# A decoder layer on one core: fillers in the router's chain, an earlier last scatter, high parts first in two units, x by two queues

## The reference

```python
h = h + HybridMixer(rms_norm(h, g1))       # gated linear attention + dilated window attention
h = h + MemXAttn(rms_norm(h, g2), mem)     # 4 heads, 256 memory tokens
h = h + MoE(rms_norm(h, g3))               # top 4 of 32 experts, router with bias
out = rms_norm(h, final_g)
```

## Time and profile before

| | us |
|---|---|
| median of 3 runs (lowest, highest) | 1241.34 (1241.11, 1243.54) |
| the profiled execution's own time | 1242.41 |
| its span, first to last instruction | 1240.7 |
| PE busy, share of the span | 1153.2, 93% |
| DVE busy | 411.6, 33% |
| ACT busy | 261.6, 21% |
| mean rate of all transfers, GB/s | 369 |
| mean granted clock of TensorE, 1 is 2.4 GHz | 0.986 |

### The profile page before, as it was taken

The page is one execution under the profiler, slowest core; times in us unless marked ns, Lnnn a source line. Parts: engine busy times, 40 slices in busy tenths (PEclk is TensorE's granted clock), DMA queues, the critical chain, the costliest instruction groups (busy, mean ns, idle before and its releaser), DMA issues.

```text
span 1240.7 us, 16139 instructions
## 1 busy us (share of the span) xinstructions
PE 1153.2 (93%) x6687; PEld 576.8 (46%) x6687; DVE 411.6 (33%) x803; ACT 261.6 (21%) x450; POOL 20.9 (2%) x40
## 2 busy tenths in 40 slices
PE   8999999999999999999989887998998898889887
PEld 7888989887433333333323232432332233224322
DVE  6789474665422222222122112211221122122112
ACT  5655464464400010010001000100110010001001
POOL 4000000000000000000000000000000000000000
PEclk9999999999899999999999999999999999999999
DMA  8455524986699999999999999999999999999996
GB/s 329 173 204 183 190 76 182 382 316 244 239 420 395 430 418 434 429 435 428 435 427 435 430 433 429 431 429 432 431 431 433 431 431 431 435 428 435 419 419 264
DMA packets 30117, 458.38 MB, mean 369 GB/s; under 512 B 3584, under 2 KB 3600, under 8 KB 8816
## 3 DMA queue, kind: packets, MB, share of 16 engines
q1 hardware_dynamic: 28800, 454.57, 87.8%
q0 software_dynamic: 832, 2.51, 0.6%
q10 hardware_dynamic: 432, 0.55, 0.1%
HBM read 456.57 MB, written 1.05 MB: 369 GB/s over the span
## 4 chain that ended last, share of the span: by engine, by line
PE 61%; DMA 29%; SPq 3%; issue 2%; ACT 2%; DVE 2%; POOL 0%; DVEq 0%; ACTq 0%; POOLq 0%
PE bank L1888 22%; DMA ring<-in_w_down 16%; DMA ring<-in_w_gate_up 12%; PE bank L1910 10%; PE bank L1495 4%; PE bank L1472 4%; PE sums L1553 3%; PE sums L1472 3%; SPq L431 3%; PE sums L1839 3%; PE sums L1495 2%; PE bank L1829 2%; PE bank L1553 2%; PE bank L1901 2%; DMA ring<-in_w_dense 1%
## 5 line engine op out<-in xcount | busy, mean ns | idle before, releaser
L1888 PE MATMUL bank<-ring,reg_a 128*64 128x512 f32 x2016 | 457.9, 606 | 42.5 <-DMA ring<-in_w_gate_up 41.8
L1888 PEld LDWEIGHTS bank<-ring,reg_a 128*64 128x64 f32 x2016 | 142.4, 139 | 324.4 <-issue 263.4
L1910 PE MATMUL bank<-ring,reg_ol 128*64 128x512 f32 x1024 | 227.0, 595 | 14.5 <-DMA ring<-in_w_down 12.8
L1389 DVE TENSOR_TENSOR masks<-bank,bT 128x256 f32<-128x256 f32 x64 | 27.2, 424 | 449.7 <-PE bank L1901 449.7
L1910 PEld LDWEIGHTS bank<-ring,reg_ol 128*64 128x64 f32 x1024 | 79.2, 137 | 141.1 <-issue 133.8
L625 ACT ACTIVATE reg_t<-bank 128x512 f32<-128x512 f32 x64 | 38.2, 597 | 440.5 <-PE bank L1888 240.5
L969 DVE SCALAR_TENSOR_TENSOR ring<-ring 128x2048 f16<-128x2048 f32 x47 | 107.3, 2289 | 40.1 <-ACT ring L643 39.8
L643 ACT ACTIVATE ring<-ring 128x2048 f16<-128x2048 f32 x47 | 89.5, 1910 | 32.7 <-PE sums L1553 14.1
L926 ACT ACTIVATE masks<-masks 128x256 f32<-128x256 f32 x64 | 26.7, 417 | 326.4 <-DVE masks L1390 326.4
L1839 PE MATMUL sums<-reg_t,reg_g 64*128 64x512 f32 x256 | 70.1, 634 | 5.5 <-ACT reg_t L625 5.5
L1376 DVE COPY reg_t<-bank 128x512 f32<-128x512 f32 x32 | 22.1, 691 | 159.2 <-PE bank L1888 159.2
(11 more groups left out here) (323 smaller groups left out, 884.8 us busy)
## 6 DMA issues: line engine op xcount, KB each, us to landing
ring<-in_w_gate_up SPq DMA_DIRECT2D x52, 4096.0 KB, 29.8
ring<-in_w_down SPq DMA_DIRECT2D x26, 4096.0 KB, 30.8
ring<-in_w_dense SPq DMA_DIRECT2D x47, 1024.0 KB, 5.1
ring<-in_w_gate_up SPq DMA_DIRECT2D x10, 2048.0 KB, 9.6
ring<-in_w_gate_up SPq DMA_DIRECT2D x16, 1024.0 KB, 25.5
ring<-in_w_down SPq DMA_DIRECT2D x6, 2048.0 KB, 11.0
ring<-in_w_gate_up SPq DMA_DIRECT2D x16, 512.0 KB, 14.2
ring<-in_w_down SPq DMA_DIRECT2D x12, 512.0 KB, 7.2
```

The costliest lines, as they stand in the source:

```text
L1888: ins = mm(pt[nh][col:col + 64, :], xg[:, c, j * SLOTS:(j + 1) * SLOTS], loaded(v + i, C, c), start=(c == 0), stop=(c == C - 1))
L1910: ins = mm(pt[2][64 * nh:64 * nh + 64, :], actT[:, 4 * i + c, :], w[:, nh * 512:(nh + 1) * 512], start=(i == 0 and c == 0), stop=(i == 1 a ...
```

## The change

1. x is loaded by two queues: SP issues the first half, ACT the second, ahead of the vectors.
2. q_g gets two banks, one for each 128 of its columns: q_g as before and q_g1, which is listed after q_g in FILLS but is given bank 7 outside the turns. PE makes q_g and q_g1 together and k_g after them by passes instead of chunks: all high by high products, then those with the low activation, then those with the low weight, each pass waiting only for the parts that it reads. DVE makes all four low parts of x_T before the second piece of the first unit's cut. ACT empties q_g and q_g1 by two copies of half the size at the old place in its stream.
3. Seven products of 128x512 that nobody reads are put into bank 0 in the router: four after the sums are opened, three after "all".
4. For the last expert both halves of the scatter of the expert before it move ahead of its first product, and the first two of its units are loaded in four pieces instead of two. Three semaphores that had been used once are counted on for pieces.
5. In the final norm DVE multiplies the second tile's half by the gain first and asks for the first root before it multiplies the first; ACT's first square no longer waits for a gain.

```diff
@@ -88 @@
-FILLS = [f"x_T{i}" for i in range(4)] + ["q_g", "k_g", "alr", "v_g0", "v_g1", "r_g0", "r_g1", "lg"]
+FILLS = [f"x_T{i}" for i in range(4)] + ["q_g", "q_g1", "k_g", "alr", "v_g0", "v_g1", "r_g0", "r_g1", "lg"]
 FILLS += [f"q_d{g}{a}" for g in range(NG) for a in range(2)] + ["cum"]
@@ -111 @@
 LAST_FILL = {k: k for k in HALVES if k in FILLS}
-LAST_FILL.update({"gla0": "bg1", "dil0": "bd1", "gla1": "bg3", "dil1": "bd3", "xv1": "xv11",
+LAST_FILL.update({"q_g": "q_g1", "gla0": "bg1", "dil0": "bd1", "gla1": "bg3", "dil1": "bd3", "xv1": "xv11",
                   "xo0": "xo01", "xo1": "xo11"})
-_N = FILLS.index("f_T0")
-BANK = {f: 4 + SUMS.index(f) if f in SUMS else i % BANKS if i < _N else (i - _N + 2) % 4 for i, f in enumerate(FILLS)}
+_TURNED = [f for f in FILLS if f != "q_g1"]
+_N = _TURNED.index("f_T0")
+BANK = {f: 4 + SUMS.index(f) if f in SUMS else i % BANKS if i < _N else (i - _N + 2) % 4 for i, f in enumerate(_TURNED)}
+BANK["q_g1"] = BANKS - 1
 TURN = {f: sum(BANK[e] == BANK[f] for e in FILLS[:i]) for i, f in enumerate(FILLS)}
@@ -336 @@
         FIRST_PIECES = {10: 4, 11: 4, 12: 4, 13: 4, 14: 2, 15: 2}
-        LAST_PIECES = {UPE * (EG - 1) + i: n for i, n in enumerate((2, 2, 4, 4, 2, 4))}
+        LAST_PIECES = {UPE * (EG - 1) + i: n for i, n in enumerate((4, 4, 4, 4, 2, 4))}
         LAST_PIECES.update({UPE * (EG - 2) + i: 2 for i in range(UPE)})
         per_group = UPE * EG
...
+        once = [spare_ld] + extra_ld
+        piece_ld = {k: (once[i], 16) if i < len(once) else (sem(f"piece_ld{k[0]}_{k[1]}"), 0)
+                    for i, k in enumerate(counted)}
...
@@ -404 @@
             xt_src = A["x"][0].rearrange("(t p) d -> p t d", p=P)
-            for t in range(TT):
-                sp.dma_start(h[:, t, :], xt_src[:, t, :]).then_inc(ld_x[t], 16)
+            sp.dma_start(h[:, 0, :], xt_src[:, 0, :]).then_inc(ld_x[0], 16)
             def columns(v, e, o, n):
@@ -619 @@
             link = chain(act, act_chain)
+            act.dma_start(h[:, 1, :], A["x"][0, P:T, :]).then_inc(ld_x[1], 16)
             act.dma_start(vT[:], A["vecs"]).then_inc(ld_ahead, 16)
@@ -680 @@
                     act.wait_ge(trig_in, 2)
-                unscaled(dst.rearrange("p a b -> p (a b)"), b[:]).then_inc(free_bank(name), 1)
+                    unscaled(dst[:, 0, :], b[:, 0:T]).then_inc(free_bank(name), 1)
+                    unscaled(dst[:, 1, :], take(act, "q_g1")[:, 0:T]).then_inc(free_bank("q_g1"), 1)
+                else:
+                    unscaled(dst.rearrange("p a b -> p (a b)"), b[:]).then_inc(free_bank(name), 1)
             b = take(act, "alr")
@@ -932 @@
                 act.wait_ge(acc_full, 2 * t + 2)
-                act.wait_ge(fin_gain, t + 1)
+                if t:
+                    act.wait_ge(fin_gain, 1)
                 act.activation(xn[:, t, :], sums[t][:], ACT.Square, accum_out=st[:, 56 + t:57 + t]).then_inc(fin_ss, 1)
                 act.wait_ge(root_done, 7 + t)
+                act.wait_ge(fin_gain, 2 - t)
                 o = out_sb[:, t, 0:512]
@@ -1022 @@
             ahead_cut(0, AHEAD, ahead_act, 1, ahead_dve)
-            for q in range(2):
+            for q in range(4):
                 low_T("x_T", q, aT, vT[:, 0:8])
             ahead_cut(AHEAD, HALF, w_high, 1, w_low)
-            for q in range(2, 4):
-                low_T("x_T", q, aT, vT[:, 0:8])
             cut_ahead("q_g")
@@ -1108 @@
             emptied(dve, "q_g")
+            emptied(dve, "q_g1")
             emptied(dve, "k_g")
@@ -1427 @@
             dve.wait_ge(ld_late, 16 * 2)
-            for t in range(TT):
-                dve.wait_ge(acc_full, 2 * t + 1)
-                gained(t, 0)
-            for t in range(TT):
-                asked(t)
+            dve.wait_ge(acc_full, 3)
+            gained(1, 0)
+            asked(0)
+            gained(0, 0)
+            asked(1)
             for t in range(TT):
@@ -1512 @@
             norm_transposes("x_T", lambda t, c: xn[:, t, c * P:(c + 1) * P], ((norm_xn, 1), (norm_xn, 2)))
-            def first_ready(c):
-                pairs_ready("x_T")(c)
-                if c == 0:
-                    pe.wait_ge(ahead_dve, 2)
-                if c == C // 2:
-                    pe.wait_ge(w_low, 1)
-            feature_major("q_g", weights("q_g"), aT, C, chunk_ready=first_ready)
-            feature_major("k_g", weights("k_g"), aT, C)
+            def highs_first(outs, w, cols, before):
+                for k, (pw, px) in enumerate(PASSES):
+                    for c in range(C):
+                        before(k, c)
+                        for b, o in zip(outs, cols):
+                            ins = mm(b, w[:, pw, c, o:o + P], aT[:, px, c, :], start=(k == 0 and c == 0),
+                                     stop=(k == 2 and c == C - 1))
+                            if k == 2 and c == C - 1 and len(outs) > 1:
+                                filled(ins, ("q_g", "q_g1")[o // P])
+                return ins
+            def cut_of(name):
+                return cut[HALVES.index(name) % EARLY].rearrange("p k (c n) -> p k c n", n=width(name))
+            def first_parts(k, c):
+                if k == 0:
+                    pe.wait_ge(x_high, c + 1)
+                    if c % (C // 2) == 0:
+                        pe.wait_ge(*((w_high, 1) if c else (ahead_act, 1)))
+                elif k == 1:
+                    pairs_ready("x_T")(c)
+                elif c % (C // 2) == 0:
+                    pe.wait_ge(*((w_low, 1) if c else (ahead_dve, 2)))
+            def second_parts(k, c):
+                if c == 0 and k == 0:
+                    pe.wait_ge(w_high, 2)
+                if c == 0 and k == 2:
+                    pe.wait_ge(w_low, 2)
+            highs_first([fill(name)[:, 0:T] for name in ("q_g", "q_g1")], cut_of("q_g"), (0, P), first_parts)
+            b = fill("k_g")
+            for i in range(2):
+                ins = highs_first([b[:, i * T:(i + 1) * T]], cut_of("k_g"), (i * P,), second_parts)
+            filled(ins, "k_g")
             pe.wait_ge(consts, 7)
@@ -1781 @@
             pe.wait_ge(f_high, 1)
+            wide = f16[:, 0, 0, 0:4, :].rearrange("p c n -> p (c n)")
+            def awake(n):
+                emptied(pe, "rl1")
+                for _ in range(n):
+                    mm(rl[1][:], f16[:, 0, 0, 0, :], wide, start=True, stop=True)
             for name in SUMS:
-                filled(mm(fill(name)[:], f16[:, 0, 0, 0, :], f16[:, 0, 0, 0:4, :].rearrange("p c n -> p (c n)"),
-                          start=True, stop=False), name)
+                filled(mm(fill(name)[:], f16[:, 0, 0, 0, :], wide, start=True, stop=False), name)
+            awake(4)
             pe.wait_ge(gate_ready, 1)
@@ -1791 @@
             filled(mm(b[:, 0:E], ones[:], mask[:, 1, :], start=False, stop=True), "all")
+            awake(3)
             def gates_T():
@@ -1856 @@
                         scatter_matrices(i)
-                    else:
+                    elif not (last and j == EG - 1):
                         scatter(j - 1, (i,))
@@ -1924 @@
                         down_biases()
+                    if last and j == EG - 1:
+                        scatter(j - 1)
                     for i in range(2):
                         between(j, i)
```

More of the change, by code:

```diff
@@ L338, in _program @@
         FIRST_PIECES = {10: 4, 11: 4, 12: 4, 13: 4, 14: 2, 15: 2}
-        LAST_PIECES = {UPE * (EG - 1) + i: n for i, n in enumerate((2, 2, 4, 4, 2, 4))}
+        LAST_PIECES = {UPE * (EG - 1) + i: n for i, n in enumerate((4, 4, 4, 4, 2, 4))}
         LAST_PIECES.update({UPE * (EG - 2) + i: 2 for i in range(UPE)})
         per_group = UPE * EG
-        piece_ld = {(v, i): sem(f"piece_ld{v}_{i}") for v, n in LAST_PIECES.items() for i in range(n)
-                    if ORDER[v % UPE][0] != 1}
+        spare_ld, extra_ld = sem("spare_ld"), [sem(f"extra_ld{i}") for i in range(2)]
+        counted = [(v, i) for v, n in sorted(LAST_PIECES.items()) for i in range(n) if ORDER[v % UPE][0] != 1]
+        once = [spare_ld] + extra_ld
+        piece_ld = {k: (once[i], 16) if i < len(once) else (sem(f"piece_ld{k[0]}_{k[1]}"), 0)
+                    for i, k in enumerate(counted)}
         def piece_done(v, i):
             m = ORDER[v % UPE][0]
-            return (piece_ld[v, i], 16) if m == 2 else (piece_ld[v - m, i], 32)
-        spare_ld, extra_ld = sem("spare_ld"), [sem(f"extra_ld{i}") for i in range(2)]
+            done, already = piece_ld[v - m % 2, i]
+            return done, already + (16 if m == 2 else 32)
         def turn_of(v, z, first):
```

## The result

The changed kernel takes 1252.1 us (median of 4 runs, 1251.86 to 1253.12) against 1241.6 of the kernel before in the same comparison: 1.0083 times, 95% interval 1.0066 to 1.0101. It is slower by about 10 us. The profiled execution took 1252.17, its span 1250.4, which is 9.7 more than before.

What follows compares the result with a forecast made beforehand. Weight transfers set the end, but PE frees their slots, so a microsecond PE loses before the first expert moves the end by one. Terms sum to +7.45 on the profiled 1242.41: 1249.9, taken as 1249.7 against the median, range 1247.0 to 1253.8.

Steps and rivals of the forecast that it cites:

- the wait for bank 7: First units: v_g0 must wait until ACT empties q_g1, behind unit 4's cut and both sines: +8.75 us.
- rival (a): Router: the stall comes and the clock falls there all the same, so no -3.0: 1252.7 us, chance 0.22.
- the half clock: After PE's wait for the bank, v_g0's products run at 1.2 GHz: +2.2 us, bounds 1.8 to 3.4.
- unit 3's late release: First units: DVE's later second cut delays unit 3's load, with unit 4 behind it: +0.5 us, bounds 0 to +1.3.
- wait at r_g1 gone: First units: PE's old idle time ahead of r_g1 disappears because PE is late: -1.15 us.
- router, with the added products: Router: the clock stays high over gathers and first expert's products, -3.0 us; the added products cost +0.1.
- smaller pieces: Last expert: two more units loaded in quarters, at a slightly lower rate: +0.2 us, bounds 0 and 0.4.
- Rival (b): Not slower: the shift of PE's first units is made up behind it by the transfer stream: 1240.1 us, chance 0.09.
- High parts first: First units: PE ends k_g near 21.8 instead of 24.3, a gain of 2.5 us that reaches nobody.
- x by two queues: First units: x one issue earlier brings DVE's second cut to some 15.4; otherwise costs or gives nothing.
- (c): Stall and more: unit 4 late by 1.3, clock low for 6.8 us, later cuts chained: 1253 to 1255, chance 0.10.
- (d): The stall, but little of the clock loss and a better router: 1247.5 us, chance 0.07.

Runs made afterwards that it cites:

- a_drain: The changed kernel, but ACT empties q_g and q_g1 right after alr's cut, ahead of the cuts of units 3 and 4 and the sines: 1243.31 us.
- a_drain_dve: a_drain with DVE again cutting the first unit's second half between the second and third pair of low parts: 1240.0 us.
- a_mem: The changed kernel with POOL's load of mem issued after the masks, the bank still emptied at the old place: 1251.05 us.
- a_nofill: The changed kernel without the seven added products: 1254.93 us.
- a_p2: The changed kernel with the first two units of the last expert in two pieces again: 1253.43 us in one run.
- b_fill: The kernel before with the seven added products alone: 1239.09 us, 0.9977 times.
- b_tail: The kernel before with the moved scatter and the new final norm alone, without the pieces: 1242.69 us in one run.
- b_x2: The kernel before with only x's second half issued by ACT's queue, ahead of the vectors: 1242.7 us for 1241.74 before.
- b_fill_tail: The kernel before with the seven added products, the moved scatter and the new final norm: 1239.83 us, 0.9985 times.
- best: The kernel before with seven products, moved scatter, new norm, later mem load, high parts first, both banks emptied early, DVE's old order; x by one queue, two pieces: 1237.87 us.

## Why the prediction was right, and where its terms were off

It forecast slower by the wait for bank 7, 1249.7 us in 1247.0 to 1253.8; 1252.1 came. Against the profiled executions the sum was +7.45 and +9.7 came. The time lies in the stated range, but 0.1 us above the narrower one of the forecast's own terms (1248.6 to 1252), and nearer to rival (a)'s 1252.7, which the traces rule out. The mechanism was right; that the time came so close is in part luck, since a term that was too large (the half clock) stands against two that were too small or missing. Each term beside what the two traces show:

| term | foreseen | shown |
|---|---|---|
| v_g0 begins later: bank 7, and unit 3's late release | +8.75 + 0.5 | 35.80 - 25.10 = +10.70 |
| v_g0 at half clock | +2.2 | +1.26 (1.8 to 2.5 in three other traces) |
| wait at r_g1 gone | -1.15 | -1.3 |
| router, with the added products | -3.0 + 0.1 | -2.73 (-1.4 to -1.5 against three other traces) |
| clock falls at 414 | none | +1.7 |
| smaller pieces | +0.2 | +0.3 (up to 0.9 in other traces) |
| final norm | -0.15 | -0.2 |
| sum | +7.45 | +9.7 |

**The bank: right.** a_drain takes away only the late copies, and 8.8 us go. Rival (b), a shift absorbed behind the wait, falls with it: a shift of 10.6 us behind r_g1 was one of 10.62 at the first gather.

**The release of unit 3: the step that was sized wrong.** The prediction said that unit 4's landing sets ACT's copies, that unit 4 stands behind unit 3, and that a load issued 1.3 us later costs between 0 and 1.3. The issue was 1.65 later (15.76), near what was worked out, and unit 4 landed only 0.3 later, inside the bounds. But unit 3 itself lands 9.06 us after its issue, and the way from it to ACT's copies, which had slack before, became the longest: DVE's low part and then its angles, to 34.69. Of the 10.70 us, 35.80 - 33.85 = 1.95 are this, by the chain; the changed kernel with DVE's old order alone was not run. The pair a_drain and a_drain_dve shows the same cut worth 3.3 us where no bank hides it. A load issued 1.6 us later landed 5.7 later with POOL's loads in the engines by then; mem's 1 MB is 2.0 of it in a_drain, and 1.03 of the 1.95 at v_g0 in a_mem. The rest is not explained by a run. The stretch of the earlier trace rows was read as room that small loads and mem fill at no cost; mem at least fills it and stays in the way. What should have been asked of the earlier trace rows is not when unit 4 is released but which of the two ways to ACT's copy has how much slack.

**The half clock after the wait: right in kind, too large.** The bounds 1.8 and 3.4 came from stretches in which PE was busy at half clock almost throughout. Here the clock fell at 28.19 inside the wait, so most of the 10.24 us cost nothing. The three other traces with the wait have 7.17 (a_mem), 7.75 (a_nofill) and 7.89 us (a_p2) for v_g0, a cost of 1.8 to 2.5, so the forecast of 2.2 fits those and the size changes from trace to trace.

**The router: right in kind, its size less sure.** It is -2.73 between the two traces, and -3.0 by b_fill's medians. But the trace before is the one with the longest fall of the four without the products: from the first gather to the second it has 6.56 us, where b_tail and b_x2 have 5.34 and a_nofill 5.19, and all ten with the products about 3.83. Against those three the products give 1.4 to 1.5 us. Rival (a), that the clock falls all the same, is in none of the ten traces with the added products. The Trainium skill (TensorE: Matmul & The Clock Gate, Part 4: PE-mode transpose) says that a transpose does not count as PE being busy in the same way; by that the fillers would have stood alone. They sufficed, so the runs do not tell whether the transposes between them helped. The prediction's "the trace disagrees" said too much: in both stretches of the earlier trace rows the granted clock is 1.00, and only the rate of the transposes rises; what raised it no run shows.

**The fall at 414: not foreseen.** It gave back 1.7 of the 2.73. It isn't the work of a part of the change: of fourteen traces it is in seven (the changed kernel, a_nofill, a_mem, b_tail, b_x2, b_fill_tail, best) and not in the other seven, always behind the same bias products. With the added products in the router it is in four traces of ten, without them in three of four, too few to say whether the two falls hang together. Since it comes and goes in kernels that differ only elsewhere, part of the 9.7 us may be chance of the one execution. That is not shown: no kernel was traced twice, and the four executions of the changed kernel have spans of 1250.1 to 1250.5.

**High parts first** gained PE 1.7 us at the end of k_g, of 2.5 foreseen; that it reaches nobody held. In a_drain it is waited away at r_g1 as well; in a_drain_dve 0.96 at v_g0 is 0.70 at r_g1. **x by two queues** was costed at nothing and costs nothing to 2 us; it was to bring DVE's second cut to 15.4, and the cut ended at 15.7, as if x had not come earlier. **Pieces and norm** came out within 0.1 us between the two traces. **The other rivals.** (c), stall and more, came in part: the stall was longer than the sum had it, but by unit 3 and not unit 4, and no later cut was waited for. (d) had the small loss by the clock right, but not a better router.

## What to carry to other kernels

Before a result is given one buffer more, look where in the reader's stream the copy stands that frees it: a fill of a few microseconds inherited a place behind two weight cuts and two sines, and stopped every later matmul. When a load is released later, follow every chain from its landing, not only the one that was longest before, and ask what else is queued for the same DMA engines; 1.6 us at the issue were 5.7 at the landing. A part of a change that is sound alone (the fillers, -3.0 by the medians) can hide behind one that is not: run them apart.

## What was unexpected of the hardware

- Eight float32 products with 32 rows (L1814 of the kernel before), 3.7 us of PE without a gap and at a granted clock of 1.0 (0.96 in a_nofill), were followed by some 3.4 us at 1.2 GHz in seven traces of fourteen. A busy PE did not protect the clock.
- All ten traces of kernels with the seven products kept the clock in the router, all four without them lost it, for 6.8 us in one and 3.4 in three (a_nofill, b_tail, b_x2).
- A small load (22 KB) issued by ACT behind half of x took 6.99 us to land, and 4.0 when it was the first in its queue.
